# Output projection of two layers: four output tiles side by side for the first six inputs, and one conv product in another PSUM bank

## The reference, cut to what matters

```
for l in range(DEPTH):                       # DEPTH = 2
    h = rmsnorm(x, norm_mix[l])
    proj = jnp.einsum('btd,de->bte', h, w_in[l])
    ...
    a_out = sliding_window_attention(q, k, v, sinks[l])
    c_out = conformer_conv(u, ug, ..., w_conv_out[l])
    merged = jax.nn.sigmoid(ga) * a_out + jax.nn.sigmoid(gb) * c_out
    x = x + jnp.einsum('btd,de->bte', merged, w_out[l])
    h2 = rmsnorm(x, norm_ffn[l])
    gu = jnp.einsum('btd,df->btf', h2, w_gate_up[l])
    ...
```

## Time and profile before

| | us |
|---|---|
| time, median of 3 runs (2336.79 to 2336.86) | 2336.82 |
| the profiled execution | 2334.86 |
| its span in the trace | 2332.6 |
| PE busy in it | 2271.0 (97%) |
| VectorE, ScalarE, GpSimd busy | 1137.1, 993.5, 981.8 |

### The profile page before, as it was taken

The page is one execution under the profiler, slowest core; times in us unless marked ns, Lnnn a source line. Parts: engine busy times, 40 slices in busy tenths (PEclk is TensorE's granted clock), DMA queues, the critical chain, the costliest instruction groups (busy, mean ns, idle before and its releaser), DMA issues.

```text
span 2332.6 us, 29198 instructions
## 1 busy us (share of the span) xinstructions
PE 2271.0 (97%) x10536; PEld 1791.9 (77%) x10560; DVE 1137.1 (49%) x1475; ACT 993.5 (43%) x1499; POOL 981.8 (42%) x453
## 2 busy tenths in 40 slices
PE   6989999999999999999999999999999999999999
PEld 5866678888888876678888888876777667888887
DVE  5876664222334785666222334647776443433300
ACT  4546643333223545744333213335535663444311
POOL 4962234444443882234444443432442113544442
PEclk9999999999999999999999999999999999999999
DMA  4321123333662221122333472322121002333332
GB/s 151 91 64 56 62 73 91 99 92 97 192 221 73 90 73 54 55 70 88 96 98 98 150 247 90 91 81 64 55 83 53 28 28 72 107 93 97 99 92 88
DMA packets 59842, 216.00 MB, mean 93 GB/s; under 512 B 6640, under 2 KB 6896, under 8 KB 59760
## 3 DMA queue, kind: packets, MB, share of 16 engines
q1 hardware_dynamic: 52272, 187.62, 26.0%
q10 hardware_dynamic: 7488, 27.27, 3.5%
HBM read 212.76 MB, written 2.10 MB: 92 GB/s over the span
## 4 chain that ended last, share of the span: by engine, by line
PE 88%; DVE 7%; ACT 4%; issue 2%; DMA 0%; SPq 0%; DVEq 0%; ACTq 0%
PE bank L1276 26%; PE bank L1278 25%; PE bank L1277 25%; PE bank L1732 1%; PE bank L1410 1%; PE bank L1289 1%; PE bank L1736 1%; PE bank L1470 1%; PE bank L1350 1%; PE bank L1450 1%; PE bank L1720 1%; PE bank L1345 1%; PE bank L1306 1%; ACT prob L479 1%; DVE root L749 1%
## 5 line engine op out<-in xcount | busy, mean ns | idle before, releaser
L307 POOL TENSOR_TENSOR wl<-raw,wh 128x1024 fp32r<-128x1024 f32 x351 | 855.7, 2438 | 1304.3 <-ACT wh L380 1304.1
L1276 PE MATMUL bank<-hh,wh 128*128 128x512 f32 x2024 | 816.3, 403 | 32.9 <-DVE hl L763 19.4
L1277 PE MATMUL bank<-hl,wh 128*128 128x512 f32 x2024 | 792.9, 392 | 0.0
L1278 PE MATMUL bank<-hh,wl 128*128 128x512 f32 x2024 | 792.8, 392 | 0.0
L380 ACT ACTIVATE wh<-raw 128x1024 fp32r<-128x1024 f32 x351 | 369.7, 1053 | 641.8 <-PE bank L1278 610.0
L1276 PEld LDWEIGHTS bank<-hh,wh 128*128 128x128 f32 x2024 | 383.1, 189 | 128.7 <-issue 28.6
L1277 PEld LDWEIGHTS bank<-hl,wh 128*128 128x128 f32 x2024 | 383.2, 189 | 86.3 <-issue 9.8
L1278 PEld LDWEIGHTS bank<-hh,wl 128*128 128x128 f32 x2024 | 382.7, 189 | 81.4
L1276 PE MATMUL bank<-ah,wh 128*128 (+1 forms) x528 | 208.0, 394 | 0.0
L1278 PE MATMUL bank<-ah,wl 128*128 (+1 forms) x528 | 207.0, 392 | 0.0
L1277 PE MATMUL bank<-al,wh 128*128 (+1 forms) x528 | 204.9, 388 | 0.0
(11 more groups left out here) (318 smaller groups left out, 2571.9 us busy)
## 6 DMA issues: line engine op xcount, KB each, us to landing
raw<-stream SPq DMA_DIRECT2D x351, 512.0 KB, 3.6
ada_w<-ada ACTq DMA_DIRECT2D x48, 512.0 KB, 4.6
x<-x_t ACTq DMA_DIRECT2D x4, 512.0 KB, 7.8
out_t<-x SPq DMA_DIRECT2D x8, 256.0 KB, 2.1
cst<-consts SPq DMA_DIRECT2D x1, 640.0 KB, 11.1
tmp<-masks SPq DMA_DIRECT2D x1, 320.0 KB, 11.3
par<-params SPq DMA_DIRECT2D x1, 253.0 KB, 4.6
cst<-consts SPq DMA_DIRECT2D x1, 224.0 KB, 8.0
```

Of the source, the lines that this page charges most:

```text
L307: nc.gpsimd.tensor_tensor(wl[:, slot, :], raw[:, raw_slot, :], wh[:, slot, :].bitcast(F32), ALU.subtract).then_inc(lo_ready, 1)
L1276: mm(dst, wh[:, slot, w], xh, start=start, stop=False)
L1277: mm(dst, wh[:, slot, w], xl, start=False, stop=False)
L1278: return mm(dst, wl[:, slot, w], xh, start=False, stop=stop)
```

## The change

`four_tiles` gets its inputs as arguments, and the first four tiles of the output projection are made by it: six inputs kk, and for each of them the products of all four tiles, into banks 0 to 3; then, tile by tile, the products with inputs 6 and 7. Tiles 4 to 7 stay as they were. The wait for `co_out` ahead of the second tile goes, and `out(6)` writes bank 5 in the place of bank 1, which is now written from the start. DVE, ACT, POOL and SP keep their instructions and order; DVE reads bank 5 for `gate_conv(6)`.

```
-                gate_conv(KT - 2, 1)
+                gate_conv(KT - 2, 5)
...
-            def four_tiles(c, banks, before):
+            def four_tiles(c, banks, xh, xl, before):
                 for kk in range(6):
                     before(kk)
                     for s, b in enumerate(banks):
                         if kk == 0:
                             pe.wait_ge(lo_ready, c + s + 1)
-                        three(bank[:, b, :], (c + s) % RW, kk, hh[:, kk, :], hl[:, kk, :], kk == 0, False)
+                        three(bank[:, b, :], (c + s) % RW, kk, xh[:, kk, :], xl[:, kk, :], kk == 0, False)
                 before(6)
                 before(7)
                 for s, b in enumerate(banks):
                     for kk in (6, 7):
-                        last = three(bank[:, b, :], (c + s) % RW, kk, hh[:, kk, :], hl[:, kk, :], False, kk == 7)
+                        last = three(bank[:, b, :], (c + s) % RW, kk, xh[:, kk, :], xl[:, kk, :], False, kk == 7)
                     last.then_inc(used, 1)
...
-                out(KT - 2, 1)
+                out(KT - 2, 5)
                 out(KT - 1, 4)
...
                 pe.wait_ge(exp_ready, 16 * l + 16)
-                for m in range(KT):
-                    if m == 1:
-                        pe.wait_ge(co_out, KT * (l + 1) - 1)
-                    if m >= 4:
-                        pe.wait_ge(x_new, 16 * l + m - 3)
+                four_tiles(c0 + C_WO, range(4), mh, ml, with_merged)
+                for m in range(4, KT):
+                    pe.wait_ge(x_new, 16 * l + m - 3)
                     c = c0 + C_WO + m
-                    tile(c, c % RW, m % 4, mh, ml, with_merged if m == 0 else lambda kk: None)
+                    tile(c, c % RW, m % 4, mh, ml)
```

More of the change, by code:

```diff
@@ L1533, in _ @@
             pe.wait_ge(x_new, XN)
-            four_tiles(CB + B_DT, [(MB + i) % 4 for i in range(4)], lambda kk: pe.wait_ge(hl_ready, 8 * N1 + kk + 1))
+            four_tiles(CB + B_DT, [(MB + i) % 4 for i in range(4)], hh, hl, lambda kk: pe.wait_ge(hl_ready, 8 * N1 + kk + 1))
             for i in range(4, XT + 1):
@@ L1786, in _ @@
             cg, pg = CB + B_GU, DEPTH * FT
-            four_tiles(cg, list(range(4)), lambda kk: pe.wait_ge(hl_ready, 8 * N2 + kk + 1))
+            four_tiles(cg, range(4), hh, hl, lambda kk: pe.wait_ge(hl_ready, 8 * N2 + kk + 1))
             with pe.Fori(1, FT // 2) as i:
```

## The result

| | kernel before | changed kernel |
|---|---|---|
| median of 6 runs each, us | 2336.84 | 2347.65 |
| the profiled execution, us | 2334.86 | 2342.36 |
| its span in the trace, us | 2332.6 | 2340.1 |

The ratio of the times is 1.0036 (95% interval 1.0025 to 1.0047), that is 2345.2 us where the kernel before takes 2336.8. The change makes the kernel slower. Ten more runs of it, against 27 runs of the kernel before, gave 1.0034 (1.0022 to 1.0046).

What follows compares the result with a forecast made beforehand. TensorE bounds the kernel, so only its standing time around the two output projections counts. Per layer 4.29 + 1.68 - 2.22 = 3.75 us more, 7.5 for both, added to 2336.82: 2344.3 us, range 2340.7 to 2346.4.

Steps and rivals of the forecast that it cites:

- What the change removes: First output tile: TensorE's wait for VectorE's `ml` of input 7 and the restart go fully, 2.22 us per layer.
- What it adds: Fourth output tile's first matmul: TensorE waits 4.29 us per layer for GpSimd's low part of that tile's chunk.
- signs of being wrong: Fourth chunk's rounding earlier than 2.7 us after the projection's start, or the fifth tile standing more than 0.3 us.
- The slow clock: Behind the fourth tile's wait: matmuls at granted clock 0.50 for about 3.5 us, 1.68 us lost per layer.
- the upper end that I had taken from 1966.55: Highest price of the slow clock: twelve matmuls after the 3.73 us idle time, 2.38 us lost per layer.
- The edits at no cost: Fifth tile's chunk, freed banks, VectorE's backlog, bank 5 for `out(6)` and the dropped `co_out` wait: nothing taken.
- VectorE's backlog: Four tiles end within 4.1 us, each costing VectorE 4.4 us at most; it catches up before the last tile.
- the fifth tile's chunk: Chunk done 4.07 us after the first tile's last matmul, wanted after 4.35; nothing taken, 0.3 us per layer at most.
- The sum: Both output projections: 4.29 + 1.68 - 2.22 = 3.75 us more per layer, 7.5 us for both.
- the clock did not hold: Rival: no slow stretch follows the 4.29 us wait, 4.4 us slower in all, 2341.2 us; chance 0.10.
- no wait at the fifth tile: Rival: fifth tile's chunk late or longer slow stretch, up to 9.5 us in all, 2346.3 us; chance 0.12.
- both waits go: Rival: fourth chunk there at 318.75, 2332.4 us; with the earliest rounding still a wait of about 1.6 us; chance 0.05.

Runs made afterwards that it cites:

- a_filled: Changed kernel with 18 more matmuls, result unread, ahead of the wait for the fourth tile's chunk; ratio 1.0013 to the kernel before.
- b_bank5: Kernel before with only the last but one conv product in bank 5 instead of bank 1; ratio 0.9996 to the kernel before.
- a_fourth_late: Changed kernel with the fourth tile's first six inputs worked off after those of the first three tiles; ratio 0.9989 to the kernel before.
- a_round_early: Changed kernel with ScalarE's rounding of the fourth tile's chunk ahead of the `mh` of input 6; ratio 1.0006 to the kernel before.

## Why the prediction was right

**What the change removes**, 2.22 us per layer: right. The wait for `ml` is gone from the list, and with three tiles side by side the projection is shorter by 2.21 and 2.23 us.

**What it adds**, 4.29 us of wait: measured 4.22 and 4.25 us (4.05 and 4.08 listed as idle). The engine, the releaser and the place were as forecast, and the chain of VectorE, ScalarE and GpSimd stood still, as the two rows of ScalarE and GpSimd show. The expectation that nothing but TensorE's position changes is what carried the whole prediction. By the letter one of the signs of being wrong was met: the rounding came 2.67 us behind the projection's start, where less than 2.7 was to count against the forecast. But that limit is the 2.71 us of the kernel before, rounded, and 0.04 us changes nothing. The prediction's "none as long as 4.29 us" leaves out the 12.0 us ahead of the first matmul of all; nothing hangs on it.

**The slow clock**, 1.68 us per layer: it came in both layers. In the second it was exactly that term, eight matmuls in 3.51 us. In the first it was thirteen matmuls and 2.72 us, more than the upper end that I had taken from 1966.55 (2.38 us). The mechanism held, its size was an undercount by 1 us. That both layers are slowed is shown by the rows, and that the slow stretch hangs on TensorE standing idle by a_filled, where 18 matmuls in the wait kept the clock at 1.00 in both layers. The price by the runs alone, 4.9 us with an uncertainty of 3.5, is too rough to tell the forecast 3.4 us from the 4.4 us of the rows. The Trainium skill's page "TensorE: Matmul & The Clock Gate" counts half of the slow time as lost ("HAM oscillation — how this bites in real kernels"): 2.85 and 1.76 us for the two stretches, against 2.72 and 1.68 from the rows. It also says, in "What's actually happening", that how many matmuls run slow differs between runs of one kernel, which is what the two layers, and the two profiled executions of the changed kernel, show (13 and 8 matmuls, then 8 and 7).

**The edits at no cost**: right for bank 5 (b_bank5), the four ends close together and VectorE's backlog (a_fourth_late), and the fifth tile's chunk, with a cover of 0.28 us that was just enough.

**The sum**: per layer 4.74 and 3.72 us were measured and 3.75 forecast; the profiled span was 2340.1 us as forecast, though partly by luck, since the 1 us too little in the first layer was offset by slow stretches that fell elsewhere. The runs are further up than the profiled execution: the ratio, 1.0036, gives 2345.2 us and lies within the range of 2340.7 to 2346.4, close to 2344.3; the median of the six runs, 2347.65, lies 1.3 us above the range. Put as a difference, 7.5 us were forecast and the ratio gives 8.4, with an interval from 5.8 to 11.0, so the agreement to 1 us is closer than the runs can tell. The term that was short is the clock. I let it vary by 0.5 us for the rest of the kernel, and single runs of one kernel vary by up to 10 us with it.

**The rivals**: the clock did not hold; of the two waits only the old one went; no wait at the fifth tile appeared. What the a_round_early run shows is that the rival "both waits go" priced its condition rightly in the first layer: with the rounding at its earliest the wait is 1.6 us. In the second it is 2.1, since GpSimd was held up by VectorE's merge.

## What to carry to other kernels

Before the work of several tiles is brought side by side to cover a late input, list for each resource that the tiles bring along (here a chunk of weights per tile) when it is ready and when it is now wanted: the cover for the one is the earlier demand for the other, and the longest of the new waits counts. Three tiles side by side cover the same late inputs as four and never ask for the late chunk.

An idle time of TensorE costs more than its length if the clock falls behind it; price it by rows of the same trace, and look at matmul durations behind each idle time, not only at the idle time.

## What the runs showed of the hardware that I had not expected

In the rows above VectorE and GpSimd exclude each other on operations that read two inputs in SBUF, in both directions. I had read only VectorE's side from the trace (2.53 and 2.98 us where 0.69 is usual). When VectorE starts first, by 0.02 us, GpSimd takes 2.88 instead of 2.4 us; when GpSimd starts first, VectorE takes 2.89 instead of 0.69 us. The Trainium skill's page "SBUF — State Buffer", section "SBUF: two separate sides", calls it an exclusive lock that the first to start holds for the whole instruction. The rows agree: in the first layer the merge ended 0.54 us after GpSimd, in the second GpSimd ended 2.21 us after the merge, so nearly the whole of the second operation (0.69 and 2.4 us alone) falls behind the end of the first.

Slow matmuls also follow short idle times, and not each time: in the changed kernel an idle time of 1.91 us was followed by a matmul of 0.79 us at 269.05, and the one of 1.92 us at the same place of its second layer by one of 0.50 us; one of 2.78 us was followed by slow matmuls at 872.40 in the kernel before and by none at the same place, 877.70, in the changed one. In the kernel before they also come where no idle time is listed at all, behind 48 matmuls of one column:

```profile
1442.67 7.33 PE L1306 MATMUL bank<-cst,ada_acc 128*128 128x1 f32 x48
1449.86 0.77 PE L1276 MATMUL bank<-hh,wh 128*128 128x512 f32 x1
```

Such differences in the clock go along with most of the difference between single runs of one kernel, 2334.9 to 2344.6 us for the kernel before with listed clocks from 0.993 to 0.988, so with a change of a few microseconds the mean clock of the runs has to be read beside the times.
